# Joining the high products of gate and up to 512 columns, and another order of the layer normalisation

## The reference

```python
def swiglu(h, w_in, w_out):                 # hidden width 2816, twice: latent and context
    a, b = jnp.split(h @ w_in, 2, axis=-1)
    return (jax.nn.silu(a) * b) @ w_out

def swiglu_2(x, wg, wu, wd):                # hidden width 2816
    return (jax.nn.silu(x @ wg) * (x @ wu)) @ wd

def layer_norm(x, g, b):                    # over the 1024 features of a token
    mu = jnp.mean(xf, -1, keepdims=True)
    var = jnp.mean(jnp.square(xf - mu), -1, keepdims=True)
    return ((xf - mu) * lax.rsqrt(var + LN_EPS) * g + b)

def rmsnorm(x, g):
    return x * lax.rsqrt(jnp.mean(x * x, axis=-1, keepdims=True) + RMS_EPS) * g
```

## Time and profile before

| | |
|---|---|
| median of the runs | 2410.09 us (2407.74 to 2412.30) |
| the profiled execution, own time | 2404.68 us |
| its span, first to last instruction | 2402.9 us |
| mean granted clock of TensorE | 0.962 |
| busy: TensorE, VectorE, ScalarE, GpSimd | 2239.5, 1279.2, 869.4, 128.0 us |
| loaded from memory | 370.64 MB, 155 GB/s over the span |

### The profile page before, as it was taken

One profiled execution on the slowest core, in us unless ns is written; L12 is line 12 of the kernel. 1 busy time (PEld: TensorE's weight loads), 2 busy tenths in 40 slices (PEclk: granted clock), 3 DMA queues, 4 the chain that ended last, 5 costly groups with the idle time before them and its releaser, 6 DMA issues. The chain is left out here.

```text
span 2402.9 us, 36377 instructions
## 1 busy us (share of the span) xinstructions
PE 2239.5 (93%) x15962; PEld 2025.1 (84%) x15962; DVE 1279.2 (53%) x1449; ACT 869.4 (36%) x891; POOL 128.0 (5%) x69
## 2 busy tenths in 40 slices
PE   6999889999999988999999979999799998789997
PEld 5887779999999657998999869998799796779996
DVE  4449635646654264556545645554555595535554
ACT  3313324334432243334333344333333344124342
POOL 0157300000000000000000000000000020000000
PEclk8999999999999999999999989999899997899998
DMA  7329704545454203554555413553355341024551
GB/s 310 107 104 394 307 0 171 185 182 182 169 191 176 96 1 121 179 190 173 195 185 182 157 53 145 188 188 144 125 190 183 132 176 71 3 79 158 192 180 48
DMA packets 52485, 373.17 MB, mean 155 GB/s; under 512 B 5728, under 2 KB 6752, under 8 KB 7840
## 3 DMA queue, kind: packets, MB, share of 16 engines
q1 hardware_dynamic: 51584, 367.78, 41.6%
q0 software_dynamic: 800, 3.93, 0.4%
HBM read 370.64 MB, written 1.05 MB: 155 GB/s over the span
## 5 line engine op out<-in xcount | busy, mean ns | idle before, releaser
L473 DVE TENSOR_TENSOR ring_r<-ring,AR_r 128x2048 fp32r<-128x2048 f32 x274 | 628.3, 2298 | 582.8 <-ACT AR_r L467 582.8
L467 ACT ACTIVATE AR_r<-ring 128x2048 fp32r<-128x2048 f32 x274 | 522.1, 1911 | 582.4 <-PE PS L370 237.8
L352 PE MATMUL PS<-AR_r 128*128 128x256 f32 x2240 | 634.1, 283 | 0.0
L354 PE MATMUL PS<-AR_r,ring_r 128*128 128x256 f32 x2240 | 633.9, 283 | 0.0
L353 PE MATMUL PS<-AR_r 128*128 128x256 f32 x2240 | 633.9, 283 | 0.0
L353 PEld LDWEIGHTS PS<-AR_r 128*128 128x128 f32 x2240 | 429.8, 192 | 2.5
L352 PEld LDWEIGHTS PS<-AR_r 128*128 128x128 f32 x2240 | 429.8, 192 | 2.5
L354 PEld LDWEIGHTS PS<-AR_r,ring_r 128*128 128x128 f32 x2240 | 429.8, 192 | 0.0
L368 PE MATMUL PS<-AR_r 128*128 128x512 f32 x616 | 240.7, 391 | 0.0
L369 PE MATMUL PS<-ring_r,AR_r 128*128 128x512 f32 x616 | 240.5, 390 | 0.0
L370 PE MATMUL PS<-AR_r 128*128 128x512 f32 x616 | 239.7, 389 | 0.0
(11 more groups left out here) (373 smaller groups left out, 3052.2 us busy)
## 6 DMA issues: line engine op xcount, KB each, us to landing
ring<-stream SPq DMA_DIRECT2D x346, 1024.0 KB, 4.8
X<-xt SPq DMA_DIRECT2D x1, 2048.0 KB, 8.3
AR<-bias POOLq DMA_DIRECT2D x1, 1536.0 KB, 6.5
AR<-pt POOLq DMA_DIRECT2D x2, 512.0 KB, 4.4
out<-X SPq DMA_DIRECT2D x1, 1024.0 KB, 4.8
SM<-small SPq DMA_DIRECT2D x1, 545.0 KB, 3.7
AR<-invc SPq DMA_DIRECT2D x1, 512.0 KB, 15.3
X<-negl POOLq DMA_DIRECT2D x1, 512.0 KB, 7.4
```

Source lines behind the costliest of these rows:

```text
L352: pe.matmul(o, w_hi, X_HI[:, k, :], start=(k == 0), stop=False)
L354: ins = pe.matmul(o, w_lo, X_HI[:, k, :], start=False, stop=(k == DT - 1))
L467: act.activation(w_hi_of(tag, i), ring[:, n % SLOTS, :], ACT.Identity).then_inc(split_hi, 1)
L473: dve.tensor_tensor(RING_R[:, n % SLOTS, :], ring[:, n % SLOTS, :], w_hi_of(tag, i), ALU.subtract).then_inc(split_lo, 1)
```

## The change

Four things are edited.

1. `gate_up`: w_hi meets X_HI and X_LO in one matmul of 512 columns. The view `X_PARTS` gives as moving operand two runs of 256 columns, one from X_HI and one from X_LO. The result fills a whole bank: columns 0 to 255 hold w_hi X_HI, to which w_lo X_HI is added, and columns 256 to 511 hold w_hi X_LO. Gate now always takes banks 6 and 7, up banks 4 and 5. TensorE waits for `ffn_gate_taken` ahead of gate and for `ffn_gated` ahead of up.
2. The halves are added behind it: ScalarE copies the low half to SBUF (`low_part`), VectorE adds the high half from PSUM. For gate this comes ahead of SiLU, which now reads SBUF; for up ahead of the multiplications. Step 0, which keeps 256 columns, has one copy of the up half on VectorE more.
3. `dve_rms_tokens`: the scaling of both tiles stands behind the statistics of both.
4. `dve_layernorm`: statistics of (0,0), (0,1), (1,0), (1,1) come ahead of both scalings, with the negated mean of tile 0 between the last two; behind a feed-forward stage the second half of chunk 1's split is done behind the second scaling.

The semaphores `inverse_turned` and `corner_zero` of mix3 are merged into others, with the same waits.

```diff
+        X_PARTS = AR_R[:, 12288:20480].rearrange("p (s n) -> p s n", s=2)
...
-            def gate_up(d, i, r):
+            def gate_up(i, step, steps, r):
 
                 for half in range(2):
                     n = n0 + i + half
                     need_split(r, i + half)
+                    if half:
+                        pe.wait_ge(ffn_gated, steps + (g0 + step))
+                    elif c or step > 1:
+                        pe.wait_ge(ffn_gate_taken, steps + (c * (FF_STEPS - 1) + step - 1))
                     for j in range(2):
-                        o = PS[:, 4 + 2 * d + half, j * T:(j + 1) * T]
+                        bank = (6, 4)[half] + j
                         for k in range(DT):
                             w = slice(k * 256 + j * P, k * 256 + (j + 1) * P)
                             w_hi, w_lo = w_hi_of(tag, i + half)[:, w], RING_R[:, n % SLOTS, w]
-                            pe.matmul(o, w_hi, X_HI[:, k, :], start=(k == 0), stop=False)
-                            pe.matmul(o, w_hi, X_LO[:, k, :], start=False, stop=False)
-                            ins = pe.matmul(o, w_lo, X_HI[:, k, :], start=False, stop=(k == DT - 1))
+                            pe.matmul(PS[:, bank, :], w_hi, X_PARTS[:, :, k * T:(k + 1) * T], start=(k == 0), stop=False, skip_group_check=True)
+                            ins = pe.matmul(PS[:, bank, 0:T], w_lo, X_HI[:, k, :], start=False, stop=(k == DT - 1), skip_group_check=True)
...
+        def dve_split_half_chunk(dve, order, tag, i, half):
+
+            n, cs = START[tag] + i, slice(half * 1024, (half + 1) * 1024)
+            dve.wait_ge(split_hi, SPLIT_BASE[tag] + i + 1)
+            ins = dve.tensor_tensor(RING_R[:, n % SLOTS, cs], ring[:, n % SLOTS, cs], w_hi_of(tag, i)[:, cs], ALU.subtract)
+            if half:
+                dve.wait_ge(order.sem, order.n)
+                ins.then_inc(split_lo, 1)
+            else:
+                ins.then_inc(order.sem, order.step())
...
-            def silu(it, r=0):
-
-                act.wait_ge(multiplied, r + (n0 + max(3 * it - 1, 0) + 1))
-                act.activation(GATE[:, it % 2, :], PS[:, 4 + 2 * (it % 2), :], ACT.Silu).then_inc(ffn_silu, 1)
-
-            def splits(it, r=0, turns=0):
-
-                for i in range(3 * it + (2 if it else 3), min(3 * it + 5, FF_CHUNKS)):
-                    act_split_chunk(act, tag, i, r, turns)
+            def silu(it, steps=0):
+
+                if it == 0:
+                    act.wait_ge(multiplied, n0 + 1)
+                    act.activation(GATE[:, 0, :], PS[:, 4, :], ACT.Silu).then_inc(ffn_silu, 1)
+                else:
+                    act.wait_ge(ffn_gate_taken, steps + (FFN_INDEX[tag] * (FF_STEPS - 1) + it))
+                    act.activation(GATE[:, it % 2, :], GATE[:, it % 2, :], ACT.Silu).then_inc(ffn_silu, 1)
+
+            def low_part(it, up, steps=0, r=0):
+                act.wait_ge(multiplied, r + (n0 + 3 * it + up))
+                if it >= 2:
+                    act.wait_ge(ffn_gated, steps + (FFN_INDEX[tag] * FF_STEPS + it - 1))
+                out, bank = (HIDDEN, 4) if up else (GATE, 6)
+                act.activation(out[:, it % 2, :].rearrange("p (j t) -> p j t", j=2), PS[:, bank:bank + 2, T:T2], ACT.Identity).then_inc(ffn_low, 1)
+
+            def splits(chunks, r=0, turns=0):
+
+                for i in chunks:
+                    if i < FF_CHUNKS:
+                        act_split_chunk(act, tag, i, r, turns)
+
+            def step(it, steps=0, r=0, turns=0):
+                low_part(it, 0, steps, r)
+                splits((3 * it + 2,), r, turns)
+                silu(it, steps)
+                low_part(it, 1, steps, r)
+                splits((3 * it + 3, 3 * it + 4), r, turns)
...
             def gating(it, steps=0, r=0):
                 d = it % 2
-                dve.wait_ge(ffn_silu, steps + (g0 + it + 1))
-
-                dve.wait_ge(multiplied, r + (n0 + (3 * it if it else 1) + 1))
+                gate, up = GATE[:, d, :], HIDDEN[:, d, :]
+                if it:
+                    dve.wait_ge(ffn_low, steps * 2 + (2 * FFN_INDEX[tag] * (FF_STEPS - 1) + 2 * it))
+                    halves_up = up.rearrange("p (j t) -> p j t", j=2)
+                    dve.tensor_tensor(halves_up, halves_up, PS[:, 4:6, 0:T], ALU.add).then_inc(ffn_hidden, 1)
+                else:
+                    dve.wait_ge(multiplied, n0 + 2)
+                    dve.tensor_copy(up, PS[:, 5, :]).then_inc(ffn_hidden, 1)
                 if it >= 2:
                     dve.wait_ge(multiplied, r + (n0 + 3 * it - 1))
-                gate, up = GATE[:, d, :], PS[:, 5 + 2 * d, :]
+                dve.wait_ge(ffn_silu, steps + (g0 + it + 1))
+                dve.wait_ge(ffn_hidden, steps * 3 + (3 * (g0 + it) + 1))
                 both = lambda ap: ap[:, d, :, :].rearrange("p a b -> p (a b)")
                 dve.tensor_tensor(both(G_HI), gate, up, ALU.mult).then_inc(ffn_hidden, 1)
-                dve.tensor_tensor(HIDDEN[:, d, :], gate, up, ALU.mult).then_inc(ffn_hidden, 1)
-                dve.wait_ge(ffn_hidden, steps * 2 + 2 * (g0 + it + 1))
+                dve.tensor_tensor(up, gate, up, ALU.mult).then_inc(ffn_hidden, 1)
+                dve.wait_ge(ffn_hidden, steps * 3 + 3 * (g0 + it + 1))
                 dve.tensor_tensor(both(G_LO), HIDDEN[:, d, :], both(G_HI), ALU.subtract).then_inc(ffn_gated, 1)
...
             def step(it, steps=0, r=0):
+                gate = GATE[:, it % 2, :].rearrange("p (j t) -> p j t", j=2)
+                dve.wait_ge(ffn_low, steps * 2 + (2 * FFN_INDEX[tag] * (FF_STEPS - 1) + 2 * it - 1))
+                dve.tensor_tensor(gate, gate, PS[:, 6:8, 0:T], ALU.add).then_inc(ffn_gate_taken, 1)
                 dve_split_chunk(dve, tag, 3 * it + 2, r)
                 gating(it, steps, r)
...
                                          op0=ALU.mult, op1=ALU.add).then_inc(S["token_stats"], S.mark("token_stats", (tag, t)))
+            for t in range(2):
                 dve.wait_ge(S["rinv"], S.at("rinv", (tag, t)))
                 dve.tensor_scalar(tok[:, t, 0:512], PS[:, banks[2 * t], :], RSTD1[s][:, t:t + 1], None, ALU.mult).then_inc(S["normed"], S.mark("normed", (tag, t)))
...
-            for i in range(2):
-                dve_split_chunk(dve, nxt, i)
-            for t in range(2):
-                for h in range(2):
-                    if (t, h) == (1, 1):
-                        need_product(dve, n_last)
-                    elif ffn or t == 0:
-                        dve.wait_ge(S["tokens_done"], S.at("tokens_done", (done, t, h)))
-                    else:
-                        need_product(dve, n_last - 2)
-                    dve.bn_stats(STATS[:, t, 6 * h:6 * h + 6], PS[:, 2 * t + h, :]).then_inc(order.sem, order.step())
+            def stats(t, h):
+
+                if (t, h) == (1, 1):
+                    need_product(dve, n_last)
+                elif ffn or t == 0:
+                    dve.wait_ge(S["tokens_done"], S.at("tokens_done", (done, t, h)))
+                else:
+                    need_product(dve, n_last - 2)
+                dve.bn_stats(STATS[:, t, 6 * h:6 * h + 6], PS[:, 2 * t + h, :]).then_inc(order.sem, order.step())
+
+            def gather(t):
+
                 dve.wait_ge(order.sem, order.n)
                 dve.bn_aggr(MEANVAR[:, t, :], STATS[:, t, :]).then_inc(S["token_stats"], S.mark("token_stats", (tag, t)))
+
+            def negate(t):
+
                 dve.wait_ge(S["rinv"], S.at("rinv", (tag, t)))
                 dve.tensor_scalar(NEGMEAN[:, t:t + 1], MEANVAR[:, t, 0:1], RSTD[:, t:t + 1], -1.0, ALU.mult, ALU.mult).then_inc(S["normed"], S.mark("normed", (tag, t, "mean")))
+
+            def scale(t):
+
                 dve.tensor_scalar(TOK[:, t, 0:512], PS[:, 2 * t, :], MEANVAR[:, t, 0:1], RSTD[:, t:t + 1], ALU.subtract, ALU.mult).then_inc(S["normed"], S.mark("normed", (tag, t)))
+
+            dve_split_chunk(dve, nxt, 0)
+            if ffn:
+                dve_split_half_chunk(dve, order, nxt, 1, 0)
+            else:
+                dve_split_chunk(dve, nxt, 1)
+            for h in range(2):
+                stats(0, h)
+            gather(0)
+            stats(1, 0)
+            negate(0)
+            stats(1, 1)
+            gather(1)
+            scale(0)
+            negate(1)
+            scale(1)
+            if ffn:
+                dve_split_half_chunk(dve, order, nxt, 1, 1)
```

More of the change, by code:

```diff
@@ L143, in build @@
         ffn_hidden = S["ffn_hidden"]
+        ffn_low = S["ffn_low"]
+        ffn_gate_taken = S["ffn_gate_taken"]
         ffn_gated = S["ffn_gated"]
@@ L498, in act_ffn @@
             n0 = START[tag]
[L500 to L508 removed]
+            def silu(it, steps=0):
[21 more added lines that the diff above has]
+                splits((3 * it + 3, 3 * it + 4), r, turns)
             act_table(act, order, ACT.Silu)
             silu(0)
[L512 removed]
+            splits((3, 4))
             if between:
@@ L517, in act_ffn @@
```

(24 more changed lines are left out.)

12 lines of the change are left out of this document (6 added, 6 removed).

## The result

In four runs each, side by side on one chip, the kernel before had a median of 2411.06 us (2407.74 to 2412.30) and the changed kernel 2380.44 us (2378.67 to 2382.27). The ratio is 0.9875, 95% interval 0.9858 to 0.9892: 30.6 us less, where the forecast had 37.4. The time lies inside the predicted range of 2361 to 2386 and 7.4 us above the predicted 2373. The profiled execution took 2382.22 us with a span of 2380.4. All medians here are of undisturbed executions; one that took 12477.59 us, of the kernel with mix0_post in the old order, is left out.

A forecast was written before the change was run, and what follows sets the result against it. TensorE's product stream was taken to bound the feed-forward stages, VectorE and ScalarE chains the boundaries. Terms -29.9 - 8.6 - 1.35 + 0.1 + 2.35 = -37.4 us took the median from 2410.09 to about 2373 us, range 2361 to 2386.

The forecast's parts named there:

- TensorE's stream is the time in the feed-forward stages: Feed-forward steps: nothing is left between TensorE's products, 16.96 us summed against 16.98 between SiLUs; other engines have room.
- The wide products, -29.9 us: Gate and up, 70 steps: 32 pairs at 240.0 ns become 512-column products at 226.7, saving 0.427 us a step.
- The price of 13.3 ns: Feed-forward matmuls: each costs about 13.3 ns besides 106.7 ns per 256 columns, whatever its width, read from the trace.
- Rival (b): Gate and up: joining a pair saves only 2.5 ns of the 13.3, total 2397 us; chance 0.03.
- Rival (a): Gate and up: the fixed 13.3 ns belongs to each run of 256 columns, products give nothing, 2402.6 us; chance 0.05.
- rival (c): Gate and up: the two-run operand is read at half rate or less, 2845 us at 440 ns a product; chance 0.04.
- The single banks, 0: Gate and up's PSUM banks: free in about 4 of 10.99 us, so TensorE never waits and the cost is zero.
- rival (d): Gate and up: single banks make TensorE wait each step; 0.15 us a step would give 2383 us; chance 0.08.
- Layer normalisation, 2.15 us at four places: Behind ffn2 to ffn5: reordering and half split start turned output at 2354.92 instead of 2357.07, 8.6 us in all.
- mix0_post, +2.35 us: Ahead of ffn0_lat: tile 0's scaling now stands behind tile 1's statistics, delaying TensorE 2.35 us, 4.5 if the clock drops.
- The clock, left out: Not summed: shorter idle may spare at most 7 us behind ffn3, ffn4, ffn5; new idle before ffn0_lat may cost 2.
- (e): Whole kernel: the forecast itself holds, within 2365 to 2381 us; chance 0.80.

The follow-up runs named there:

- mix0_post in the old order: Changed kernel, but mix0_post's second stream again scales tile 0 ahead of tile 1's statistics: 2380.52 us, ratio 0.9878 to the kernel before.
- wide meets wide: Changed kernel with gate's 16 wide products before its 16 narrow ones, up's narrow before wide: 2370.46 us, ratio 0.9836 to the kernel before.
- one run: Changed kernel with X_HI and X_LO interleaved, so a wide product reads 512 unbroken columns: 2380.39 us, ratio 0.9873 to the kernel before.
- grouped with one run: Changed kernel with X_HI and X_LO interleaved and, per bank, eight wide then eight narrow products: 2377.48 us, ratio 0.9866 to the kernel before.
- grouped: Changed kernel with eight wide products, then eight narrow ones, for each bank: 2374.81 us, ratio 0.9852 to the kernel before.
- normalisations only: Kernel before with the new order of both normalisations and the half split, gate and up products unchanged: 2398.24 us, ratio 0.9948.
- products only: Changed kernel with both normalisations in the old order and no half split: 2396.12 us, ratio 0.9938 to the kernel before.

## Why the prediction was right, and the term that was off

**TensorE's stream is the time in the feed-forward stages.** Right. Apart from the clock in ffn0_ctx each change of the products' prices shows in the stage to 0.1 us, and what ScalarE and VectorE got besides cost nothing.

**The wide products, -29.9 us.** The mechanism was right and the size was off: 6 x 2.09 + 1.86 = 14.4 us. The step that failed is "I take 226.7, the row with the same type, width and kind of product". That row was taken in the middle of a run of 24 equal products. In the changed kernel each wide product stands between narrow ones, and a pair costs 352.5 ns instead of 346.7: 32 x 5.8 = 0.19 us a step. The down products behind take 5.50 us instead of the sum's 5.44: the mean distances of the first ten are 240, 237, 233, 236, 224, 231, 236, 228, 232 and 231 ns, then 227. Together about 0.25 us a step; measured is 16.79 - 16.55 = 0.24. The sign of it could be seen before: a down's first five distances there had a mean of 233, 236, 228, 232 and 231 ns behind 256-column products, and the first two distances of the 256s behind a down 113 and 119. The prediction read only the later ones. One change to 512 columns and back costs about 27 - 8 = 19 ns by these, which is the 0.02 us between the prediction's 16.96 and the 16.98 of the earlier trace rows. That widths are the cause is shown by wide meets wide; that it is not the two-run operand by one run, and by grouped with one run. It is not the other engines' work: grouped and wide meets wide have the same. What in TensorE makes a change of width cost, no run shows.

**The price of 13.3 ns and the Trainium skill's 2.5.** Rival (b) went by the 2.5 ns fixed cost that the Trainium skill ("TensorE: Matmul & The Clock Gate", section Back-to-back issue gap) gives for the isolated gap between two matmuls. Wide meets wide agrees with the trace's 13.3 ns instead: it saves 175.09 - 170.88 = 4.2 us a stage, where 32 x 10 x 13.3 ns are 4.3. Rival (a), a fixed cost per run of 256 columns, and rival (c), a slower read of two runs, fall with it.

**The single banks, 0.** Right, rival (d) falls: no product waits for a bank.

**Layer normalisation, 2.15 us at four places.** Right: 2.23 us behind each of ffn2 to ffn5 (8.82 to 6.59 us), and with normalisations only the same. That the last product is what is late next is not shown: tile 0's negated mean comes 0.12 us ahead of its end. Behind ffn1_lat 1.35 us was forecast, 1.6 measured (8.73 to 7.14 us); with normalisations only it is 1.2. The 0.1 us of mix2 and mix3 is too small to be seen.

**mix0_post, +2.35 us.** Right: +2.30. The clock that might cost 2 there cost 1.4 in the changed kernel's trace.

**The clock, left out.** It gave back 2.45, 2.13 and 2.22 us behind ffn3, ffn4 and ffn5, 6.8 us of the "at most 7", and took 1.4 us at ffn0_lat and 1.5 behind ffn1_lat (11.92 to 13.38 us). So a part of the missing 15 us came from a term that the prediction had named but not summed. That is luck: the terms that it did sum, as measured, are 14.4 + 8.9 + 1.6 - 2.3 = 22.6 us, which from 2410.09 leads to 2387.5 us, outside the range. The 4.5 us of clock bring it to 2383.0, inside.

**The sum.** From ffn0_lat's first product to the end the profiled executions differ by 29.1 us. The terms are 14.4 of products, 8.9 and 1.6 of normalisation, and 4.5 of clock (6.8 - 1.4 - 1.5, and 0.6 gained at the start of ffn1_lat), 29.4 in all; mix1 and mix2 between, whose products the change doesn't touch, take 1.1 us more and 0.8 less. In products only they take 1.3 and 2.9 us more. Ahead of that product the changed kernel's execution was 6.6 us later: 2.3 is the order, 4.3 is the difference ahead of tile 0's statistics, which executions of the same code show too (4.8 us between before and products only). It is why this pair of profiles shows 22.5 us where the medians show 30.6. What makes that start part vary was not looked into.

**Slips in the working.** The chances of (a), (b), (d) and (e) add to 0.96, where 0.95 is written, and (c)'s 2845 starts from 2404.7 where (a) and (b) start from 2410.1. Neither moves the forecast.

## What to carry to other kernels

A price per matmul read in the middle of a run of equal products holds only for such runs: read the distances at the start of a run too, and keep products of one width together (and the last of one group at the width of the next). When an order of work is changed in a function with several callers, go to each caller and ask who waits for the piece that now comes later; one place here lost 2.3 us. Test the parts alone and also together, since the clock behind a boundary can turn on both.

## What the runs showed of the hardware

- Where widths alternate, a matmul of 512 columns costs 235.9 ns to the next start and one of 256 116.6, together 5.8 ns more than the 226.7 and 120.0 of long runs. A run of 512s behind a run of 256s has 233, 236, 228, 232 and 231 ns and then 227 (before, grouped, wide meets wide); behind alternating widths it needs ten matmuls.
- A moving operand in two runs of 256 columns, 16 KB apart, is as fast as one run of 512 (173.00 us a stage in both, and 171.46 in both where eight come together).
- Behind boundaries of 8.8 us the granted clock was about 0.5 (1.2 GHz) in the kernel before. Behind those of 6.6 us it was 1.00 in the changed kernel, and in others with the same 6.6 us but other products ahead 0.62 to 0.69 at two or all three of the places. With products only, one gap of 8.82 us (behind ffn4) has 11.46 us behind it, the time at full clock. The length of the gap, in which TensorE only turns the tiles, doesn't decide it alone.
